# A layer norm whose mean, squares and sums are begun while its last inputs are still being made

## The reference, cut to what matters

```python
def layer_norm(x, g, b):                       # LN_EPS = 1e-5
    mu = jnp.mean(xf, axis=-1, keepdims=True)
    var = jnp.mean(jnp.square(xf - mu), axis=-1, keepdims=True)
    y = (xf - mu) * lax.rsqrt(var + LN_EPS)
    return y * g + b

mix = hybrid_mixer(x, ...)                     # ends with merged @ w_o
x = layer_norm(alpha * x + mix, ln1_g, ln1_b)  # the norm of this case
ff = swiglu_ffn(x, w_gate, w_up, w_down)       # silu(x @ gate) * (x @ up) @ down
x = layer_norm(alpha * x + ff, ln2_g, ln2_b)
```

## Time and profile before

| what | us |
|---|---|
| median of 3 runs (908.15 to 911.45) | 909.68 |
| the profiled execution | 914.21 |
| its span, first to last instruction | 912.4 |
| last `wo` matmul to first feed-forward matmul | 701.25 to 716.64 |

### The profile page before, as it was taken

One profiled execution on the slowest core, in us unless ns is written; L12 is line 12 of the kernel. 1 busy time (PEld: TensorE's weight loads), 2 busy tenths in 40 slices (PEclk: granted clock), 3 DMA queues, 4 the chain that ended last, 5 costly groups with the idle time before them and its releaser, 6 DMA issues.

```text
span 912.4 us, 13258 instructions
## 1 busy us (share of the span) xinstructions
PE 882.4 (97%) x5318; PEld 715.3 (78%) x5318; DVE 627.9 (69%) x1243; ACT 442.7 (49%) x753; POOL 21.2 (2%) x16
## 2 busy tenths in 40 slices
PE   7999999999999999999999999999998999999996
PEld 4568477767687777877998888899998888888885
DVE  5432766585845759866699999978586766655666
ACT  3351515544623355554544444566553665555552
POOL 0000000000000000000002212000000000000000
PEclk9998999999999999999999999999999999999999
DMA  9674452100263033204455555432466155555551
GB/s 356 265 296 183 172 210 69 47 24 1 93 252 123 13 127 139 84 21 139 164 185 185 185 188 182 154 125 70 121 197 215 61 194 180 182 192 205 169 179 47
DMA packets 39997, 136.68 MB, mean 150 GB/s; under 512 B 4352, under 2 KB 4480, under 8 KB 39680
## 3 DMA queue, kind: packets, MB, share of 16 engines
q1 hardware_dynamic: 38928, 130.48, 41.9%
q10 hardware_dynamic: 1008, 5.36, 1.5%
HBM read 134.77 MB, written 1.05 MB: 149 GB/s over the span
## 4 chain that ended last, share of the span: by engine, by line
PE 82%; DVE 13%; ACT 3%; DMA 1%; issue 1%; SPq 0%; DVEq 0%; ACTq 0%
PE ps L392 9%; PE ps L929 6%; PE ps L349 5%; PE ps L350 5%; PE ps L432 4%; PE ps L434 4%; PE ps L433 4%; PE ps L393 4%; PE ps L354 4%; PE ps L704 3%; PE ps L462 2%; DVE wlo L1432 2%; PE ps L377 2%; PE ps L727 2%; PE ps L366 2%; PE ps L379 2%
## 5 line engine op out<-in xcount | busy, mean ns | idle before, releaser
L1432 DVE TENSOR_TENSOR wlo<-raw,whi 128x1024 fp32r<-128x1024 f32 (+2 forms) x204 | 232.1, 1158 | 35.1 <-ACT whi L967 35.0
L967 ACT ACTIVATE whi<-raw 128x1024 fp32r<-128x1024 f32 (+2 forms) x204 | 204.1, 1005 | 92.0 <-DMA raw<-wpack 39.6
L349 PE MATMUL ps<-hx,whi 128*128 128x256 f32 (+1 forms) x400 | 121.0, 303 | 0.5 <-DVE hx L2023 0.5
L392 PE MATMUL ps<-hx,whi 128*128 128x512 f32 x336 | 119.5, 398 | 0.0
L350 PE MATMUL ps<-hx,whi 128*128 128x256 f32 (+1 forms) x400 | 117.3, 293 | 0.0
L354 PE MATMUL ps<-hx,wlo 128*128 128x256 f32 (+1 forms) x346 | 101.6, 294 | 0.0
L393 PE MATMUL ps<-hx,wlo 128*128 128x256 f32 x336 | 94.3, 281 | 0.0
L349 PEld LDWEIGHTS ps<-hx,whi 128*128 128x128 f32 x400 | 76.4, 191 | 4.8 <-issue 1.9
L350 PEld LDWEIGHTS ps<-hx,whi 128*128 128x128 f32 x400 | 76.5, 191 | 2.3 <-issue 0.7
L392 PEld LDWEIGHTS ps<-hx,whi 128*128 128x128 f32 x336 | 63.1, 188 | 15.2
L432 PE MATMUL ps<-whi,hx 128*128 128x512 f32 (+1 forms) x192 | 72.2, 376 | 0.2 <-ACT acc L1033 0.2
(11 more groups left out here) (278 smaller groups left out, 1698.8 us busy)
## 6 DMA issues: line engine op xcount, KB each, us to landing
raw<-wpack SPq DMA_DIRECT2D x178, 512.0 KB, 4.1
AF<-wmod SPq DMA_DIRECT2D x48, 512.0 KB, 6.3
raw<-wpack SPq DMA_DIRECT2D x24, 256.0 KB, 3.2
XT<-xin SPq DMA_DIRECT2D x4, 512.0 KB, 6.0
raw<-wpack SPq DMA_DIRECT2D x4, 432.0 KB, 6.6
uq<-wuq ACTq DMA_DIRECT2D x2, 768.0 KB, 5.5
cst<-cpack ACTq DMA_DIRECT2D x1, 1093.0 KB, 7.9
AF<-wukv ACTq DMA_DIRECT2D x2, 512.0 KB, 6.8
```

What stands on the lines that cost most here:

```text
L349: e.matmul(o, wh[:, b], xh(k), start=j == 0, stop=False, skip_group_check=True)
L392: e.matmul(ps.ap(key, 512).rearrange("p (s n) -> p s n", s=2), wh[:, b], K.hx[:, :, k, 0:256], start=k == 0, stop=False, skip_group_check= ...
L967: e.activation(W.hi(i), W.raw(i), ACT.Copy).then_inc(*HI.up(j))
L1432: e.tensor_tensor(W.lo(i), W.raw(i), W.hi(i), ALU.subtract).then_inc(*LO.up(j))
```

## The change

The running sum leaves VectorE: GpSimd adds the tiles as they come. After the fourth tile has been added (and output 4 has been multiplied), TensorE sums `acc` with ones (`"c"`), and ScalarE scales by 1/512: the mean of half the features. With this preliminary mean `c` tiles are centred by VectorE and squared by ScalarE between the outputs: tiles 0 to 2 after output 5, tiles 3 to 6 after output 6, tile 7 after output 7. GpSimd adds up the squares as well (`sqsum`), so that TensorE needs two matmuls for the full sum (`"m"`) and two for the squares (`"v"`). VectorE then forms `d` = mean - `c`, its square, and takes the variance as the mean square about `c` minus `d` squared. GpSimd subtracts `d` from the eight tiles (L2155), while VectorE computes 1/sqrt; the multiplication by the gain now waits for GpSimd's tile as well.

```diff
--- before.py
+++ after.py
@@ -326,7 +326,7 @@
 
 
 def tensor_program(K, e):
-    pe, M, A, V, LO, W, ps, C = Eng(e), K.mm, K.act, K.dve, K.lo, K.W, K.ps, K.C
+    pe, M, A, V, G, LO, W, ps, C = Eng(e), K.mm, K.act, K.dve, K.pool, K.lo, K.W, K.ps, K.C
     hh, hl = K.hh, K.hl
 
     def weights(key, desc, n, split=True):
@@ -802,7 +802,7 @@
         gi, w = late.pop(0)
         for t in range(2):
             key = ("tT", gi, w, t)
-            pe.wait_ge(K.pool["turn", gi, w, t], *ps.take(key))
+            pe.wait_ge(G["turn", gi, w, t], *ps.take(key))
             for j in range(4):
                 i = e.transpose(ps.ap(key, P, j * P), g.rot[:, t * 1024 + j * P:t * 1024 + (j + 1) * P], C("ident"))
             i.then_inc(*M.up(key))
@@ -897,20 +897,21 @@
             i.then_inc(*M.up(("ao", m + y)))
         W.given[c] = M.now()
 
+    def ln1_sum(what, *parts):
+
+        key = ("ln1", what)
+        free = ps.take(key)
+        for j, (x, there) in enumerate(parts):
+            pe.wait_ge(there, *free)
+            i = e.matmul(ps.ap(key, 256), C("ones"), x, start=j == 0, stop=j == len(parts) - 1, skip_group_check=True)
+        i.then_inc(*M.up(key))
+
     for m in range(KD):
         lin(("wo", m), "w_o_2", 0, (P * m, P), range(KD), x2h, x2l, 256, lambda k: V["mg", k])
-
-    def ln_sums(nm):
-
-        pe.wait_ge(V[nm, "acc"], *ps.take((nm, "m")))
-        e.matmul(ps.ap((nm, "m"), 256), C("ones"), K.acc[:, 0:256], start=True, stop=True, skip_group_check=True).then_inc(*M.up((nm, "m")))
-        pe.wait_ge(*ps.take((nm, "v")))
-        for k in range(KD):
-            pe.wait_ge(A[nm, "sq", k])
-            z = k % 4 * 256
-            e.matmul(ps.ap((nm, "v"), 256), C("ones"), K.sq[:, z:z + 256], start=k == 0, stop=k == KD - 1, skip_group_check=True).then_inc(*M.up((nm, "v", k)))
-
-    ln_sums("ln1")
+        if m == 4:
+            ln1_sum("c", (K.acc[:, 0:256], G["x1sum", 3]))
+    ln1_sum("m", (K.acc[:, 0:256], G["x1sum", 6]), (K.XT[:, 7, XC], V["x1", 7]))
+    ln1_sum("v", (K.x1[0], G["sqsum", 6]), (K.sq[:, 768:1024], A["x1sq", 7]))
     keep(11)
     xt3 = lambda k: V["x3", k]
 
@@ -953,7 +954,7 @@
 
 
 def scalar_program(K, e):
-    ac, M, A, V, HI, W, ps, C = Eng(e), K.mm, K.act, K.dve, K.hi, K.W, K.ps, K.C
+    ac, M, A, V, G, HI, W, ps, C = Eng(e), K.mm, K.act, K.dve, K.pool, K.hi, K.W, K.ps, K.C
     hh, hl, XT = K.hh, K.hl, K.XT
     done = [0]
 
@@ -1359,20 +1360,25 @@
             highs(("ao", m))
         ac.wait_ge(V["mgs", m], M["attn2"])
         e.activation(hh[:, m, 0:256], g.Gt[:, m, :], ACT.Copy, scale=0.5).then_inc(*A.up(("mg", m)))
+    def x1_square(m):
+        z = m % 4 * 256
+        ac.wait_ge(V["x1c", m], G["sqsum", m - 4] if m >= 5 else G["sqsum", 1] if m == 4 else None)
+        e.activation(K.sq[:, z:z + 256], K.x1[3] if m == 7 else XT[:, m, XC], ACT.Square).then_inc(*A.up(("x1sq", m)))
+
     for m in range(KD):
         highs(("wo", m))
+        if m == 5:
+            ac.wait_ge(M["ln1", "c"])
+            e.activation(K.mean[:, :], ps.ap(("ln1", "c"), 256), ACT.Copy, scale=1.0 / 512).then_inc(*A.up(("ln1", "c")))
+            ps.give(("ln1", "c"), A.now())
+            for k in range(3):
+                x1_square(k)
+        if m == 6:
+            for k in range(3, 7):
+                x1_square(k)
     e.dma_start(K.AF[:, 3072:5120], K.l2rows).then_inc(*K.l2_in.up("rows"))
 
-    def ln_sums(nm):
-        ac.wait_ge(M[nm, "m"])
-        e.activation(K.mean[:, :], ps.ap((nm, "m"), 256), ACT.Copy, scale=1.0 / D).then_inc(*A.up((nm, "m")))
-        ps.give((nm, "m"), A.now())
-        for k in range(KD):
-            z = k % 4 * 256
-            ac.wait_ge(V[nm, "c", k], M[nm, "v", k - 4] if k >= 4 else None)
-            e.activation(K.sq[:, z:z + 256], XT[:, k, XC], ACT.Square).then_inc(*A.up((nm, "sq", k)))
-
-    ln_sums("ln1")
+    x1_square(7)
 
     def x3(k):
         z = k % 4 * 256
@@ -1418,7 +1424,7 @@
 
 
 def vector_program(K, e):
-    dv, M, A, V, HI, LO, W, ps, C = Eng(e), K.mm, K.act, K.dve, K.hi, K.lo, K.W, K.ps, K.C
+    dv, M, A, V, G, HI, LO, W, ps, C = Eng(e), K.mm, K.act, K.dve, K.pool, K.hi, K.lo, K.W, K.ps, K.C
     hh, hl, XT = K.hh, K.hl, K.XT
     done = [0]
 
@@ -2034,25 +2040,32 @@
             merge_low(m - 1)
     merge_low(KD - 1)
 
+    def x1_centre(m):
+
+        dv.wait_ge(A["ln1", "c"], V["x1", m], G["x1sum", max(m, 1)] if m < 7 else None)
+        e.tensor_tensor(K.x1[3] if m == 7 else XT[:, m, XC], XT[:, m, XC], K.mean[:, :], ALU.subtract).then_inc(*V.up(("x1c", m)))
+
     for m in range(KD):
         lows(("wo", m))
         dv.wait_ge(M["wo", m])
-        e.scalar_tensor_tensor(out=XT[:, m, XC], in0=XT[:, m, XC], scalar=ALPHA, in1=ps.ap(("wo", m), 256), op0=ALU.mult, op1=ALU.add).then_inc(*V.up())
+        e.scalar_tensor_tensor(out=XT[:, m, XC], in0=XT[:, m, XC], scalar=ALPHA, in1=ps.ap(("wo", m), 256), op0=ALU.mult, op1=ALU.add).then_inc(*V.up(("x1", m)))
         ps.give(("wo", m), V.now())
-        add_up(XT[:, m, XC], m == 0, ("ln1", "acc"), M["cn2", "s"])
-
-    def ln_wide(nm):
-        dv.wait_ge(A[nm, "m"])
-        for k in range(KD):
-            e.tensor_tensor(XT[:, k, XC], XT[:, k, XC], K.mean[:, :], ALU.subtract).then_inc(*V.up((nm, "c", k)))
-        v, y, w = K.rs[:, 0:256], K.rs[:, 256:512], K.acc[:, 0:256]
-        dv.wait_ge(M[nm, "v", KD - 1])
-        e.tensor_scalar(v, ps.ap((nm, "v"), 256), 1.0 / D, LN_EPS, ALU.mult, ALU.add).then_inc(*V.up())
-        ps.give((nm, "v"), V.now())
-        rsqrt(v, y, w)
-        return v
-
-    r = ln_wide("ln1")
+        for k in {5: (0, 1, 2), 6: (3, 4, 5, 6), 7: (7,)}.get(m, ()):
+            x1_centre(k)
+
+    r, y, w = K.rs[:, 0:256], K.rs[:, 256:512], K.acc[:, 0:256]
+    d, d2 = K.x1[1], K.x1[2]
+    dv.wait_ge(M["ln1", "m"])
+    e.scalar_tensor_tensor(out=d, in0=ps.ap(("ln1", "m"), 256), scalar=1.0 / D, in1=K.mean[:, :], op0=ALU.mult, op1=ALU.subtract).then_inc(*V.up("x1d"))
+    ps.give(("ln1", "m"), V.now())
+    dv.wait_ge(V.now())
+    e.tensor_tensor(d2, d, d, ALU.mult).then_inc(*V.up())
+    dv.wait_ge(V.now())
+    e.tensor_scalar(d2, d2, LN_EPS, None, ALU.subtract, ALU.bypass).then_inc(*V.up())
+    dv.wait_ge(M["ln1", "v"], V.now())
+    e.scalar_tensor_tensor(out=r, in0=ps.ap(("ln1", "v"), 256), scalar=1.0 / D, in1=d2, op0=ALU.mult, op1=ALU.subtract).then_inc(*V.up())
+    ps.give(("ln1", "v"), V.now())
+    rsqrt(r, y, w)
 
     def x3_low(k):
         z = k % 4 * 256
@@ -2062,7 +2075,7 @@
     dv.wait_ge(V.now())
     for k in range(KD):
         z = k % 4 * 256
-        dv.wait_ge(A["x3", k - 4] if k >= 4 else None, V.now())
+        dv.wait_ge(A["x3", k - 4] if k >= 4 else None, V.now(), G["x1m", k])
         e.scalar_tensor_tensor(out=K.sq[:, z:z + 256], in0=XT[:, k, XC], scalar=C("l1g", k, 1), in1=r, op0=ALU.mult, op1=ALU.mult).then_inc(*V.up(("x3t", k)))
         if k:
             x3_low(k - 1)
@@ -2111,13 +2124,35 @@
 
 def gpsimd_program(K, e):
 
-    gp, V, rot = Eng(e), K.dve, K.G[2].rot
+    gp, A, V, G, rot = Eng(e), K.act, K.dve, K.pool, K.G[2].rot
     for gi in range(3):
         for w in range(2):
             for t in range(2):
                 a, b = rot[:, t * 1024:t * 1024 + 512], rot[:, t * 1024 + 512:t * 1024 + 1024]
                 gp.wait_ge(V["parts", gi, w, t])
-                e.tensor_tensor(a, a, b, ALU.add).then_inc(*K.pool.up(("turn", gi, w, t)))
+                e.tensor_tensor(a, a, b, ALU.add).then_inc(*G.up(("turn", gi, w, t)))
+
+    x, acc = (lambda m: K.XT[:, m, XC]), K.acc[:, 0:256]
+
+    def x1_sum(m):
+        gp.wait_ge(V["x1", m], G.now(), K.mm["ln1", "c"] if m == 4 else None)
+        e.tensor_tensor(acc, x(0) if m == 1 else acc, x(m), ALU.add).then_inc(*G.up(("x1sum", m)))
+
+    def sq_sum(m):
+        z = m % 4 * 256
+        gp.wait_ge(A["x1sq", m], G.now())
+        e.tensor_tensor(K.x1[0], K.sq[:, 0:256] if m == 1 else K.x1[0], K.sq[:, z:z + 256], ALU.add).then_inc(*G.up(("sqsum", m)))
+
+    for m in range(1, 6):
+        x1_sum(m)
+    for m in range(1, 3):
+        sq_sum(m)
+    x1_sum(6)
+    for m in range(3, 7):
+        sq_sum(m)
+    gp.wait_ge(V["x1d"])
+    for k in range(KD):
+        e.tensor_tensor(x(k), x(k) if k < 7 else K.x1[3], K.x1[1], ALU.subtract).then_inc(*G.up(("x1m", k)))
 
 
 def sync_program(K, e):
@@ -2200,6 +2235,7 @@
         K.sq, K.rs = K.wk[:, 0:1024], K.wk[:, 1024:1536]
         K.acc = sb("acc", [P, 512])
         K.mean = K.acc[:, 256:512]
+        K.x1 = [K.AF[:, 9216 + 256 * i:9472 + 256 * i] for i in range(4)]
         K.mod = sb("mod", [P, 96])
         K.modrow = sb("modrow", [P, 512])
         K.nrm = sb("nrm", [P, 12])
```

## The result

The change makes the kernel slower: the ratio of the runs after to those before is 1.0026, with a 95% interval of 1.0014 to 1.0037, and the medians are 912.98 and 910.62 us (14 runs each). In a later comparison it was 1.0017 (1.0002 to 1.0032). The forecast was 908.9, hardly any change, and the range 904.5 to 912.3; the time lies above the range. Of the 4.1 us between 912.98 and 908.9, 0.9 is the level of before itself (910.62 here, 909.68 in the three runs that I forecast from), 0.8 the gain that I forecast and 2.4 the loss that came in its place. The change is still within the 0.3% that I had called likeliest.

What follows compares the result with a forecast made beforehand. TensorE was taken to bound the kernel, with a 15.07 us norm chain where it waits. Shortening gave 6.7 us, turns left 1.4, half clock took 0.6: 909.68 - 0.8 = 908.9 us, range 904.5 to 912.3.

Steps and rivals of the forecast that it cites:

- the 0.3% that I had called likeliest: Whole kernel: time within 0.3% (2.7 us) of before, chance 0.59; faster by more 0.27, slower 0.14.
- The mechanism of the turns: Norm: GpSimd and VectorE instructions each reading two SBUF operands alternate whole instructions; GpSimd's turn at 256 columns about 0.55 us.
- the walk at full clock: Changed norm, step by step with turns: output 7 written at 704.54, 1/sqrt 5.6 us, ending at 713.5.
- the sum: Whole kernel: gain of 0.8 us taken from the profiled 914.21 and from the median 909.68, giving 913.4 and 908.9.
- The walk's gain of 1.4 at full clock: End of 1/sqrt at 713.5 against 714.95 before, with TensorE at full clock: 1.4 us gained.
- the 0.6 us for half clock on the changed kernel's sums: TensorE's second `m` matmul and two `v` matmuls: 0.2 us a pass slower, some 0.6 on the path, leaving 0.8.
- The half clock itself: TensorE standing from 702.5 to 705.0 ahead of output 7's matmul: clock expected to fall again, previously for 6.8 us.
- No turns here: Norm: 256-column instructions of GpSimd and VectorE pass each other, 6.7 us faster, 903.0; with half-way cases, chance 0.27.
- The clock falls at the wrong place: Start of the feed-forward part at half clock: loses 2.0 us, net 0.6 slower, 910.3; chance 0.15.
- GpSimd's turns are long: Centrings 3 to 6 and 1/sqrt: each 0.1 us more per turn costs 1.4; 912.1 at 0.8; chance 0.14.
- Its limit of 0.64: GpSimd's turn at 256 columns: from 0.64 us on, the forecast gain is gone.

Runs made afterwards that it cites:

- later comparison: The changed kernel, unedited, timed again against the kernel before: 912.55 us, ratio 1.0017 (1.0002 to 1.0032).
- the first profile: The changed kernel's first profiled execution, nothing further edited: 910.5 us, 31.01 us from output 1 to the first feed-forward matmul.
- with fillers: Kernel before plus two filler matmuls ahead of the sum over features and three ahead of the sums of squares: 909.65 beside 909.75 us, ratio 0.9995.
- the third execution of the changed kernel: The changed kernel, unedited, profiled a third time: 30.93 us from output 1 to the first feed-forward matmul, 39.75 to the next chunk.

## Why the prediction was wrong

**The mechanism of the turns held.** Counted from output 1, the walk at full clock put output 7 at 20.25 us (measured 20.18), 1/sqrt at 5.6 us (5.68 at full clock, with six instructions held as forecast) and its end at 29.2 (29.25). Each held instruction was longer by 0.41, where the walk had 0.42. In the first profile 1/sqrt took 5.11, since it began later and only five were held.

**The step that failed** is the sum: "914.21 - 0.8 = 913.4 for the profiled execution, and for the median 909.68 - 0.8 = 908.9". It carries a gain over one execution to the median. The gain came from sixteen passes at 0.42 us, and I had noted that this was the clock and had even the price at full clock, 0.22. Sixteen passes at that are 3.6 and not 6.79 us; measured with fillers they are 3.72, and the norm before takes 29.29 us from output 1 and not 32.35, 3.1 less. The walk's gain of 1.4 at full clock is then a loss of 1.7, and 1.65 was measured. The walk for the changed kernel was made at full clock and corrected for the clock, that for the old kernel never was.

The profiled execution was 4.5 us above the median, a sign that it wasn't the usual course, and none of before's 69 runs timed beside the later kernels was as slow. The sign pointed at two places: against the profile with fillers (907.78) it was 6.4 us slow, of which 3.4 lay ahead of output 1 and 3.1 in the norm.

**A second term was off**, the 0.6 us for half clock on the changed kernel's sums. With half clock there the first feed-forward matmul came at 31.01 and 30.92, without it at 30.94: it costs under 0.1, since 1/sqrt in any case ends only after GpSimd's last subtraction. The gain against the profiled execution was therefore 1.34 us up to the first feed-forward matmul and not 0.8. That it was 0.83 at the next chunk is luck: half clock in the first tiles, which the sum had left out, took the other 0.5. The half clock itself was forecast for 6.8 us from the pause ahead of output 7's matmul; there it came for 3.4 us, in two of three executions.

**The rivals.** "No turns here" is refuted: 0.83 against 0.42 in 1/sqrt, back to 0.42 without GpSimd's subtractions or with an operand in PSUM. "The clock falls at the wrong place" is what the third execution of the changed kernel shows in full, at 1.5 us for the 2.0 I gave, and the first in part (0.5); it adds to the loss. "GpSimd's turns are long" is wrong: a 256-column addition takes 0.73 alone, and a turn costs VectorE 0.41 in a chain as forecast. (Its limit of 0.64 starts from the gain of 1.4; from the 0.8 of the sum the same 1.4 us for each 0.1 gives 0.61.) None of them was the cause: none had asked what before costs at full clock, which should have been the rival on the other side.

Not settled is how the 2.4 us between the medians divide: 1.65 is the norm at equal clock, the rest is within what clock and scatter can make.

## What to carry to other kernels

A gain that is made of matmuls at half clock is gone wherever an execution doesn't meet the fall; here 1.3 us against one execution was a loss of 1.65 at equal clock. Price both kernels at full clock first, then the clock for each, and look whether the profiled execution is near the median. Work handed to GpSimd doesn't run freely beside VectorE instructions with two operands in SBUF (0.83 for 0.42 us); with one of VectorE's operands in PSUM it did. If a sum is moved off TensorE to GpSimd and something waits for it, compare the two: here 0.45 us on TensorE against 0.88 from one of GpSimd's sums to the next.

## What the runs showed of the hardware that was not expected

A `tensor_scalar` of 256 columns from SBUF to SBUF, with one input, is held beside GpSimd's subtractions like one with two (0.85 for 0.29), which the prediction's own rows didn't show. Where VectorE's chain runs beside a fixed row of GpSimd instructions, a start 0.6 us earlier ended it only 0.1 earlier (variance at 23.75 and 23.11 us from output 1, end of 1/sqrt at 29.32 and 29.24). TensorE's clock fell at 713.4 in the changed kernel's first profile after a stretch whose only pause was 1.67 us, between the filler and the first feed-forward tile; in the earlier trace rows it had been two pauses of 0.97 and 1.38.
